# Splits ahead of the gate's chain in head 0, and the norm weight's turn behind x tile 0

## The chip, the cores and the metric

The kernel runs on one core of one Trainium2 chip. The metric is the device time of one execution in microseconds. Before the change the median of three runs is 1736.66 us (1736.09 to 1736.99).

The engines are called TensorE (PE; PEld is its weight load), VectorE (DVE), ScalarE (ACT), GpSimd (POOL) and SyncE (SP). They run side by side, each takes its own instructions in order, and they meet through semaphores.

## The reference, cut to what matters

One layer: RMSNorm, forgetting attention with a residual, RMSNorm, SwiGLU with a residual, and a last RMSNorm. 512 tokens, width 2048, 4 heads of 256, all in float32. This case touches the first norm, the projections of head 0 and the decay of the attention:

```
h    = rmsnorm(x, norm_mix)
proj = h @ w_in                       # q, k, v of 1024 columns each, and 4 gate columns
f    = proj[..., 3*A:] + b_f
cum  = cumsum(log_sigmoid(f), axis=tokens)
logits = (q @ k.T) * HEAD_DIM**-0.5 + cum[t] - cum[s]      # s <= t
o    = softmax(logits) @ v ; x = x + merge(o) @ w_out
```

## The kernel before, in words

**Two parts of each number.** A float32 product is made of three passes over a high and a low part of each operand (fp32r). ScalarE writes the high part as a copy (`split_hi`, L915, instruction at L919), VectorE the low part as raw less high (`split_lo`, L1342, L1344). A **slab** is 128 columns of a weight, 2048 rows deep; `raw` has three places and `split` two. Slab n goes to place n mod 2 of `split`, so its split waits until slab n - 2 is used (`slab_used`), and SP's queue loads slab n + 3 when slab n is split (`lo_ready`).

**Head 0's slabs** are 0 and 1 (q), 2 and 3 (k), 4 and 5 (v). TensorE projects each in 48 matmuls (`project`, L1942; all matmuls of a product have the line L1907) into one of two banks in turn. `take_qk` empties the bank of a q or k slab: VectorE multiplies it in place by the row of roots (L1410; for v the product goes to `vT`), ScalarE copies the high part (L961), VectorE makes the low part (L1419). TensorE's projection j waits for the slab's low part and for take_qk j - 2.

**The opening** (TensorE from L2030, ScalarE from L1007, VectorE from L1458). POOL sets constants. TensorE keeps itself busy with four matmuls (L2017), turns the norm weight's rows (L2034) into a bank, and ScalarE copies that to `gain_col` (L1010, `gain_taken`); this bank is also that of the last two of the 16 chunks of the turned x, so TensorE waits for `gain_taken` ahead of these. `turn_x` (L1924, L1934) turns a tile of 128 tokens of x in 16 transposes; two tiles make a half (EARLY, LATE) of 256 tokens, which ScalarE and VectorE take chunk by chunk, scaled by `gain_col`, into high (`take_x`, L931) and low part (L1358). ScalarE squares each x tile for the root mean square (`square_x`, L1002). The gate's columns `wf` are spread over `pad` in high (L1017) and low part (L1454), and `gate` (L2025) makes the gate's columns out of 16 matmuls for each half. Slab 0 is split in four pieces (L1021, L1459; `first_lo` counts the low ones) and projected for the early half, then the late one; then come slab 1's tiles, with the turn of the row of roots in between (L2058), whose result VectorE copies to `root_row` (L1527).

**The gate's chain** in head 0: `gate_sums` on VectorE, a DMA that moves rows down 16 partitions (`gate_moved`, issued by ScalarE at L1030), then in `gate_decay` (L1489) on VectorE sums, root and bias (L1493 to L1498, `gate_v` 3 to 5), on ScalarE `gate_softplus` (L988: Abs, Exp, Ln with a load of a table), on VectorE minimum, cumulative sum and the two parts of the decay (L1500 to L1517), and `decay_h` (L1431). The scores (`scores`, L1951) need `decay_ready` and four take_qk.

**Who sets the order.** Every engine's order is written out by hand. For head 0 the functions `head` are called with `before=None` (`fresh`); the other heads run in a loop of three, with the work of the head before them between the steps. Behind the heads come w_out, the second norm, and the feed-forward part by Strassen-like products, which takes most of the time.

Of the kernel before, what the change touches and what calls it, by code (L numbers as in the profile page):

```python
# [23 lines left out]
ALU = mybir.AluOpType  # L24
# [148 lines left out]
def fox_layer(nc, x, norm_mix, w_in, b_f, w_out, norm_ffn, w_gu, w_down, norm_out, out):  # L173
# [38 lines left out]
    with ExitStack() as ctx:  # L212
# [6 lines left out]
        def f32(ap):  # L219
            return ap.bitcast(F32)  # L220
# [693 lines left out]
        def _(act):  # L914
# [19 lines left out]
            def softmax(h):  # L934
                for tb in range(NT):
                    act.wait_ge(max_ready, NT * h + (tb + 1))
                    nc.scalar.activation(tmp_row(tb), ps[:, SC[tb], 0:(tb + 1) * P], ACT.Exp,
                                         bias=negmax[:, tb:tb + 1],
                                         accum_out=rowsum[:, tb:tb + 1]).then_inc(exp_done, 1)
# [19 lines left out]
            def take_qk(h, at, j):  # L959
                act.wait_ge(rescaled, QK * h + (j + 1))  # L960
                nc.scalar.activation(qk[j // NH][0][:, j % NH, :], ps[:, PROJ[j % 2], :], ACT.Copy,  # L961
                                     scale=SCALE if j < NH else 1.0).then_inc(qk_hi, 1)

            def head(at, h, before=None):

                fresh = before is None
                if not fresh:
                    split_hi(at.plus(1))
                    softmax(before)
                take_qk(h, at, 0)  # L970
                split_hi(at.plus(2))
                if fresh:
                    gate_softplus()
                if not fresh:
                    take_v(before)
                take_qk(h, at, 1)
                split_hi(at.plus(3))
                if not fresh:
                    take_pT(before)
                take_qk(h, at, 2)  # L980
                split_hi(at.plus(4))
                if not fresh:
                    take_o(before)
                take_qk(h, at, 3)
                split_hi(at.plus(5))
                split_hi(at.plus(6))
# [21 lines left out]
            act.dma_start(gain_rows[0:ND, :], norm_mix.rearrange("a (c p) -> (a c) p", p=P)).then_inc(gain_in, 16)  # L1008
            act.wait_ge(gain_turned, 1)
            nc.scalar.activation(gain_col[:], ps[:, SC[3], 0:ND], ACT.Copy).then_inc(gain_taken, 1)  # L1010
            square_x(0)
            act.wait_ge(gain_taken, 1)
            take_x(0, range(0, 4))
# [4 lines left out]
            take_x(0, range(4, ND))  # L1018
# [322 lines left out]
        def _(dve):  # L1341
# [79 lines left out]

            def head(at, h, head_col, before=None):
                fresh = before is None
                if not fresh:
                    split_lo(at.plus(1))
                    softmax(before)
                take_qk(h, at, 0)
                split_lo(at.plus(2))
                if fresh:
                    gate_decay()  # L1430
                nc.vector.tensor_scalar(decay_h[:], f32(decay_s[:]), head_col, None,  # L1431
                                        ALU.mult).then_inc(decay_ready, 1)
                if not fresh:
                    take_v(before)
                take_qk(h, at, 1)
                split_lo(at.plus(3))
                if not fresh:
                    take_pT(before)
                take_qk(h, at, 2)
                split_lo(at.plus(4))  # L1440
                if not fresh:
                    take_o(before)
                take_qk(h, at, 3)
                split_lo(at.plus(5))
                take_v_rows(h, at, 0)
                split_lo(at.plus(6))
                take_v_rows(h, at, 1)
# [3 lines left out]
            take_x(0, range(0, 4))  # L1451
# [4 lines left out]
            take_x(0, range(4, ND))  # L1456
# [32 lines left out]
            def gate_decay():  # L1489
# [8 lines left out]
                nc.vector.tensor_scalar(z, z, bf[:, 0:1], None, ALU.add).then_inc(gate_v, 1)  # L1498
                dve.wait_ge(gate_s, 3)
# [22 lines left out]
            for tb in range(NT):  # L1522
                dve.wait_ge(rstd_ready, tb + 1)
                nc.vector.tensor_scalar(vT[:, 0, tb * P:(tb + 1) * P], warm[:, 0:P], rstd[:, tb:tb + 1], None,
                                        ALU.add).then_inc(root_spread, 1)
            dve.wait_ge(root_turned, 1)
# [375 lines left out]
        def _(pe):  # L1902
# [129 lines left out]
            pe.wait_ge(const_set, IDENT)  # L2032
            pe.wait_ge(gain_in, 16)
            nc.tensor.transpose(ps[:, SC[3], 0:P], gain_rows, ident[:]).then_inc(gain_turned, 1)  # L2034
            turn_x(0, range(0, ND - 2))
# [6 lines left out]
            turn_x(2, range(0, 2 * FIVE))  # L2042
            for j in range(2):
                pe.wait_ge(first_lo, j + 1)
                project(first, PROJ[0], EARLY, range(4 * j, 4 * j + 4), wait=False)
            turn_x(3, range(0, 2 * FIVE))
            pe.wait_ge(first_lo, 3)
            project(first, PROJ[0], EARLY, range(8, 12), wait=False)
            project(first, PROJ[0], EARLY, range(12, ND))
# [5 lines left out]
            project(first.plus(1), PROJ[1], tiles=range(0, ND // 2))  # L2055
# [4 lines left out]
            project(first.plus(1), PROJ[1], tiles=range(ND // 2, ND)).then_inc(slab_used, 1)  # L2060
# [225 lines left out]
```

## Time and profile before

| | us |
|---|---|
| median of three runs | 1736.66 |
| the profiled run | 1736.89 |
| its span | 1735.1 |
| TensorE busy | 1713.1 (99%) |
| VectorE busy | 1214.6 (70%) |
| ScalarE busy | 780.3 (45%) |
| GpSimd busy | 174.7 (10%) |

Times in the views are microseconds from the start of the span. A busy TensorE isn't TensorE at its peak: matmuls are pipelined, the next starts before the last has ended, so the distance of two starts counts, not the duration of one. The granted clock is given as a share of 2.4 GHz; 0.50 is 1.2 GHz, and a value between says that the clock changed in that stretch. A line of the order of time merges like instructions: start, time from the first start to the last end, engine, line, operation, count, and in brackets how long the engine sat idle ahead of it and who ended that.

### The profile page before, as it was taken

How to read it: one execution, taken by the hardware profiler on the slowest of the kernel's cores; microseconds unless marked ns; L12 is line 12 of the kernel's file. 1: busy time of each engine (PE TensorE's matmuls, PEld its weight loads, DVE VectorE, ACT ScalarE, POOL GpSimd, SP SyncE). 2: the span in 40 equal slices, each digit the busy share in tenths (PEclk: the TensorE clock that was granted, in tenths of full speed). 3: DMA queues.
4: the chain of work that ended last, by engine and by line, in shares of the span. 5: the costliest groups of instructions: out<-in, count | busy, mean ns of one | idle time of the engine just before them, and what ended most of it. 6: DMA issues, size and time to landing. Idle time of an engine off the chain costs nothing.

```text
span 1735.1 us, 24508 instructions
## 1 busy us (share of the span) xinstructions
PE 1713.1 (99%) x8861; PEld 1465.5 (84%) x8861; DVE 1214.6 (70%) x1323; ACT 780.3 (45%) x956; POOL 174.7 (10%) x276
## 2 busy tenths in 40 slices
PE   9899999999999999999999999999999999999997
PEld 7688888888988888888888888888887888888886
DVE  4533434335877777777777777777779978888886
ACT  5222222233344544455454545445455544445454
POOL 1000000000001111111111111111100100000043
PEclk9999999999999999999999999999999999999999
DMA  7233332252347777776777777777778886876854
GB/s 225 73 97 79 91 79 91 73 206 61 92 126 199 180 181 187 205 195 176 186 187 193 181 180 181 208 195 178 184 231 237 255 244 197 249 188 190 254 156 143
DMA packets 306437, 296.44 MB, mean 171 GB/s; under 512 B 9425, under 2 KB 258529, under 8 KB 300753
## 3 DMA queue, kind: packets, MB, share of 16 engines
q1 hardware_dynamic: 288704, 223.67, 42.0%
q0 software_dynamic: 15120, 65.54, 19.6%
q10 hardware_dynamic: 2560, 6.53, 1.1%
q8 instruction: 34, 0.56, 0.1%
q14 instruction: 19, 0.15, 0.0%
HBM read 202.68 MB, written 27.26 MB: 133 GB/s over the span
## 4 chain that ended last, share of the span: by engine, by line
PE 95%; DVE 2%; ACT 1%; issue 1%; POOL 0%; DVEq 0%; POOLq 0%; ACTq 0%
PE ps L2159 30%; PE ps L2210 24%; PE ps L1907 20%; PE ps L2165 16%; PE ps L2143 2%; PE ps L2148 1%; DVE tmp L1369 1%; PE ps L2125 1%; PE ps L2025 1%; PE ps L2017 0%; PE ps L2129 0%; PE ps L1934 0%; DVE split L1344 0%; PE ps L1979 0%; DVE hT L1350 0%
## 5 line engine op out<-in xcount | busy, mean ns | idle before, releaser
L1096 ACT ACTIVATE split<-raw 128x1024 fp32r<-128x1024 f32 x295 | 312.1, 1058 | 342.5 <-DVE raw L1602 112.9
L1591 DVE TENSOR_TENSOR split<-raw,split 128x1024 fp32r<-128x1024 f32 x295 | 360.5, 1223 | 139.0 <-ACT split L1096 134.9
L2210 PE MATMUL ps<-split,operand_hi 128*128 128x512 f32 x1232 | 380.7, 389 | 1.0 <-DVE operand_lo L1746 0.8
L1907 PE MATMUL ps<-hT,split 128*128 128x512 f32 (+1 forms) x1200 | 268.3, 384 | 6.9 <-DVE split L1344 6.9
L2210 PEld LDWEIGHTS ps<-split,operand_hi 128*128 128x128 f32 x1232 | 231.3, 188 | 50.9 <-DVE operand_lo L1746 1.2
L1907 PEld LDWEIGHTS ps<-hT,split 128*128 128x128 f32 x1200 | 219.6, 189 | 50.8 <-issue 7.7
L2159 PE MATMUL ps<-hT,split 128*128 128x512 f32 x984 | 246.4, 392 | 0.0
L2210 PE MATMUL ps<-split,operand_lo 128*128 128x512 f32 x616 | 239.7, 389 | 0.0
L1196 ACT ACTIVATE split<-down_slot 128x2048 fp32r<-128x2048 f32 (+1 forms) x84 | 148.6, 1774 | 179.9 <-PE ps L2210 86.8
L2159 PEld LDWEIGHTS ps<-hT,split 128*128 128x128 f32 x984 | 177.0, 189 | 31.7
L1732 DVE TENSOR_TENSOR split<-down_slot,split 128x2048 fp32r<-128x2048 f32 (+1 forms) x84 | 177.2, 2109 | 20.9 <-ACT split L1196 17.4
L2159 PE MATMUL ps<-oT,split 128*128 128x512 f32 x656 | 164.3, 392 | 0.0
L2165 PEld LDWEIGHTS ps<-hT,split 128*128 128x128 f32 x984 | 134.2, 190 | 9.6
L2165 PE MATMUL ps<-hT,split 128*128 128x256 f32 x984 | 137.2, 282 | 0.0
L2159 PEld LDWEIGHTS ps<-oT,split 128*128 128x128 f32 x656 | 118.0, 189 | 21.1
L2210 PEld LDWEIGHTS ps<-split,operand_lo 128*128 128x128 f32 x616 | 115.7, 188 | 23.8
L1757 DVE TENSOR_TENSOR xres<-xres,ps 128x1024 f32<-128x1024 f32 (+1 forms) x74 | 88.0, 1189 | 42.8 <-PE ps L2210 42.4
L1344 DVE TENSOR_TENSOR split<-raw,split 128x2048 fp32r<-128x2048 f32 x33 | 75.6, 2292 | 53.9 <-ACT split L919 53.9
L1602 DVE TENSOR_TENSOR raw<-raw 128x1024 f32<-128x1024 f32 x83 | 101.7, 1226 | 7.8
L814 POOL TENSOR_TENSOR turn_of<-half 128x1 f32<-128x1 f32 x81 | 31.4, 388 | 740.4 <-DVE raw L1602 316.4
L919 ACT ACTIVATE split<-raw 128x2048 fp32r<-128x2048 f32 x33 | 63.0, 1914 | 84.5 <-PE ps L1907 80.9
L2165 PEld LDWEIGHTS ps<-oT,split 128*128 128x128 f32 x656 | 89.5, 190 | 6.4
(184 smaller groups left out, 1927.7 us busy)
## 6 DMA issues: line engine op xcount, KB each, us to landing
raw<-in_ffn_w_gate_up_dram SPq DMA_DIRECT2D x172, 512.0 KB, 4.8
raw<-raw POOLq DMA_DIRECT2D x81, 512.0 KB, 4.5
down_slot<-in_ffn_w_down_dram SPq DMA_DIRECT2D x32, 1024.0 KB, 7.0
raw<-in_fox_w_in_dram SPq DMA_DIRECT2D x24, 1024.0 KB, 5.7
a_sums<-pack SPq DMA_DIRECT2D x22, 1024.0 KB, 6.3
down_slot<-down_slot POOLq DMA_DIRECT2D x16, 1024.0 KB, 7.6
operand_raw<-a_sums SPq DMA_DIRECT2D x28, 512.0 KB, 6.4
down_slot<-in_ffn_w_down_dram SPq DMA_DIRECT2D x16, 768.0 KB, 5.4
```

Of the source, the lines that this page charges most:

```text
L919: nc.scalar.activation(split[0][:, at.ring, :], raw[:, at.raw, :], ACT.Copy).then_inc(hi_ready, 1)
L1096: nc.scalar.activation(ring(r, 0, n), source, ACT.Copy).then_inc(t_hi, 1)
L1196: nc.scalar.activation(down_ring(dn, 0, e), down_part(dn, DOWN_OF[e]), ACT.Copy).then_inc(d_hi, 1)
L1344: nc.vector.tensor_tensor(split[1][:, at.ring, :], raw[:, at.raw, :], f32(split[0][:, at.ring, :]), ALU.subtract).then_inc(lo_ready, 1)
L1591: nc.vector.tensor_tensor(ring(r, 1, n), source, f32(ring(r, 0, n)), ALU.subtract).then_inc(t_lo, 1)
L1602: nc.vector.tensor_tensor(x1, x1, x2, ALU.add).then_inc(t_sum, 1)
L1732: nc.vector.tensor_tensor(down_ring(dn, 1, e), down_part(dn, DOWN_OF[e]), f32(down_ring(dn, 0, e)), ALU.subtract).then_inc(d_lo, 1)
L1757: nc.vector.tensor_tensor(part, part, down_banks(dn, which)[:, tiles, :], ALU.add if sign > 0 else ALU.subtract).then_inc(y_added, 1)
L1907: ins = nc.tensor.matmul(bank, stationary(sp, t), moving(mp, t), start=first and t == tiles[0] and (sp, mp) == PASSES[0], stop=last and t ...
L2159: ins = nc.tensor.matmul(both, ring(at.r, 0, n)[:, k * P:(k + 1) * P], tokens[2][:, :, k * HALF:(k + 1) * HALF], start=e < 2 and k == 0, s ...
L2165: ins = nc.tensor.matmul(both[:, 0, :], ring(at.r, 1, n)[:, k * P:(k + 1) * P], tokens[0][:, k * HALF:(k + 1) * HALF], start=False, stop=k ...
L2210: ins = nc.tensor.matmul(banks[:, tile, :], operand[e][part][:, i, tile * P:(tile + 1) * P], down_ring(dn, part_of_t, e)[:, i * BANK:(i + ...
```

## The change

Six moves, no work added or taken away:

1. TensorE turns chunks 0 to 13 of x tile 0 ahead of the norm weight, not behind it.
2. ScalarE squares x tile 0 ahead of its copy to `gain_col`; ScalarE and VectorE take two chunks ahead of the pads, not four.
3. TensorE projects pieces j = 0 and 1 of slab 0 ahead of ten transposes of x tile 2 and 3 each, not behind tile 2's.
4. The row of roots is turned behind ten tiles of slab 1, not eight.
5. In head 0 slab 2 is split ahead of take_qk 0, on VectorE ahead of the copy to `root_row` too.
6. The gate's chain goes in two parts: `gate_logits` and ScalarE's `gate_softplus` behind the split of slab 3, the rest (`gate_decay`, and `decay_h`) behind the split of slab 4. Both stood behind slab 2's split, ahead of take_qk 1.

```diff
 # ScalarE, head
+                if fresh:
+                    split_hi(at.plus(2))
                 take_qk(h, at, 0)
-                split_hi(at.plus(2))
-                if fresh:
-                    gate_softplus()
                 if not fresh:
+                    split_hi(at.plus(2))
                     take_v(before)
                 take_qk(h, at, 1)
                 split_hi(at.plus(3))
+                if fresh:
+                    gate_softplus()
 # ScalarE, opening
+            square_x(0)
             act.wait_ge(gain_turned, 1)
             nc.scalar.activation(gain_col[:], ps[:, SC[3], 0:ND], ACT.Copy).then_inc(gain_taken, 1)
-            square_x(0)
             act.wait_ge(gain_taken, 1)
-            take_x(0, range(0, 4))
+            take_x(0, range(0, 2))
...
-            take_x(0, range(4, ND))
+            take_x(0, range(2, ND))
 # VectorE, head
                 take_qk(h, at, 0)
-                split_lo(at.plus(2))
-                if fresh:
-                    gate_decay()
-                nc.vector.tensor_scalar(decay_h[:], f32(decay_s[:]), head_col, None,
-                                        ALU.mult).then_inc(decay_ready, 1)
                 if not fresh:
+                    split_lo(at.plus(2))
+                    decay_of(head_col)
                     take_v(before)
                 take_qk(h, at, 1)
                 split_lo(at.plus(3))
+                if fresh:
+                    gate_logits()
...
                 split_lo(at.plus(4))
+                if fresh:
+                    gate_decay()
+                    decay_of(head_col)
 # VectorE, opening (its two take_x as ScalarE's), and the gate
-            def gate_decay():
+            def gate_logits():
...
                 nc.vector.tensor_scalar(z, z, bf[:, 0:1], None, ALU.add).then_inc(gate_v, 1)
+            def gate_decay():
+
+                dve.wait_ge(gate_v, 5)
                 dve.wait_ge(gate_s, 3)
...
+            split_lo(At(2))
             dve.wait_ge(root_turned, 1)
 # TensorE, opening
+            turn_x(0, range(0, ND - 2))
             pe.wait_ge(gain_in, 16)
             nc.tensor.transpose(ps[:, SC[3], 0:P], gain_rows, ident[:]).then_inc(gain_turned, 1)
-            turn_x(0, range(0, ND - 2))
...
-            turn_x(2, range(0, 2 * FIVE))
-            for j in range(2):
-                pe.wait_ge(first_lo, j + 1)
+            for j in range(4):
+                pe.wait_ge(first_lo if j < 3 else lo_ready, j + 1 if j < 3 else 1)
                 project(first, PROJ[0], EARLY, range(4 * j, 4 * j + 4), wait=False)
-            turn_x(3, range(0, 2 * FIVE))
-            pe.wait_ge(first_lo, 3)
-            project(first, PROJ[0], EARLY, range(8, 12), wait=False)
-            project(first, PROJ[0], EARLY, range(12, ND))
+                if j < 2:
+                    turn_x(2 + j, range(0, 2 * FIVE))
...
-            project(first.plus(1), PROJ[1], tiles=range(0, ND // 2))
+            project(first.plus(1), PROJ[1], tiles=range(0, 10))
...
-            project(first.plus(1), PROJ[1], tiles=range(ND // 2, ND)).then_inc(slab_used, 1)
+            project(first.plus(1), PROJ[1], tiles=range(10, ND)).then_inc(slab_used, 1)
```

## Rows read from the trace of the kernel before

**Rows 1.** The page: the chain that ended last, and the group of projection matmuls.
```profile
PE 95%; DVE 2%; ACT 1%; issue 1%; POOL 0%; DVEq 0%; POOLq 0%; ACTq 0%
...
L1907 PE MATMUL ps<-hT,split 128*128 128x512 f32 (+1 forms) x1200 | 268.3, 384 | 6.9 <-DVE split L1344 6.9
```

**Rows 2.** TensorE's waits: total us, times, longest us.
```profile
PE ps L1907 <- DVE split L1344: 6.9, 2, 6.0
...
PE ps L2210 <- DVE operand_lo L1746: 0.8, 1, 0.8
```

**Rows 3.** TensorE in order of time, 30 to 110 us.
```profile
43.08 5.73 PE L1907 MATMUL ps<-hT,split 128*128 128x512 f32 x24
49.70 11.16 PE L1907 MATMUL ps<-hT,split 128*128 128x512 f32 x48 [0.89 <-DVE split L1344]
...
66.89 35.09 PE L1907 MATMUL ps<-hT,split 128*128 128x512 f32 x144 [6.04 <-DVE split L1344]
101.82 0.22 PE L1907 MATMUL ps<-kT_hi,qT_hi 128*128 128x128 f32 x1
```

**Rows 4.** TensorE by stretches: busy (count), granted clock, DMA share, GB/s.
```profile
13.00:14.00 1.00, 0.72 (x2) 0.76 0.96 388
...
16.52:48.60 32.08, 32.08 (x205) 0.99 0.60 157
...
64.00:65.00 1.00, 0.00 (x0) 0.86 0.00 0
...
71.00:72.00 1.00, 1.00 (x5) 0.72 1.03 251
```

**Rows 5.** VectorE and ScalarE in order of time, 43 to 67 us.
```profile
51.43 0.63 ACT L991 ACTIVATE tmp<-tmp 128x512 f32<-128x512 f32 x1 [4.21 <-DVE tmp L1498]
...
62.52 1.90 ACT L919 ACTIVATE split<-raw 128x2048 fp32r<-128x2048 f32 x1
...
43.37 0.69 DVE L1527 COPY root_row<-ps 128x512 f32<-128x512 f32 x1 [5.19 <-PE ps L2058]
...
47.26 2.29 DVE L1344 TENSOR_TENSOR split<-raw,split 128x2048 fp32r<-128x2048 f32 x1 [1.11 <-ACT split L919]
49.47 0.68 DVE L1493 TENSOR_TENSOR tmp<-tmp 112x512 f32<-112x512 f32 x1
...
54.70 0.69 DVE L1500 SCALAR_TENSOR_TENSOR tmp<-tmp 128x512 f32<-128x512 f32 x1 [3.31 <-ACT tmp L995]
...
61.30 0.69 DVE L1410 TENSOR_TENSOR ps<-ps,root_row 128x512 f32<-128x512 f32 x1
...
64.45 2.29 DVE L1344 TENSOR_TENSOR split<-raw,split 128x2048 fp32r<-128x2048 f32 x1 [1.11 <-ACT split L919]
```

**Rows 6.** TensorE in order of time, 0 to 20 us.
```profile
7.62 3.66 PE L1934 MATMUL ps<-ident,xres 128*128 128x128 f32 x32
13.28 5.50 PE L2025 MATMUL ps<-hT,oT 128*128 128x512 f32 x16 [2.00 <-DVE oT L1454]
18.61 1.25 PE L1934 MATMUL ps<-ident,xres 128*128 128x128 f32 x10
```

**Rows 7.** ScalarE and VectorE in order of time, 0 to 20 us.
```profile
7.82 0.18 ACT L1010 ACTIVATE gain_col<-ps 128x16 f32<-128x16 f32 x1 [4.67 <-PE ps L2034]
...
9.85 1.57 ACT L931 ACTIVATE hT<-ps,gain_col 128x256 fp32r<-128x256 f32 x4
...
10.80 1.66 DVE L1358 SCALAR_TENSOR_TENSOR hT<-ps,gain_col,hT 128x256 fp32r<-128x256 f32 x4 [10.80 <-ACT hT L931]
...
17.79 2.49 DVE L1459 TENSOR_TENSOR split<-raw,split 128x512 fp32r<-128x512 f32 x4
```

**Rows 8.** DMAs, us to landing: x's first two loads, all four, the norm weight's.
```profile
xres<-in_x_dram SPq DMA_DIRECT2D x2, 1024.0 KB, 6.1
...
DMA to landing us min/median/max: 5.0/7.6/8.6
...
tmp<-in_norm_mix_dram ACTq DMA_DIRECT2D x1, 8.0 KB, 5.3
```

More of the change, by code:

```diff
@@ L1420, in take_qk, with decay_of @@
                                                ALU.mult, ALU.subtract).then_inc(qk_done, 1)
+            def decay_of(head_col):
+                nc.vector.tensor_scalar(decay_h[:], f32(decay_s[:]), head_col, None,
+                                        ALU.mult).then_inc(decay_ready, 1)
             def head(at, h, head_col, before=None):
@@ L1450, in _ @@
             dve.wait_ge(gain_taken, 1)
-            take_x(0, range(0, 4))
+            take_x(0, range(0, 2))
             for r in range(4):
@@ L1455, in _ @@
                                         ALU.subtract).then_inc(pad_lo, 1)
-            take_x(0, range(4, ND))
+            take_x(0, range(2, ND))
             for j in range(4):
```

## The prediction

> **What bounds the kernel now.** I read the chain of waits first: TensorE carries 95% of it [rows 1], so only time in which TensorE waits or runs slowly can be won. Next, the waits of TensorE: two waits of its projections for VectorE's splits make 6.9 us, the longest 6.0, and the others after the opening are under a microsecond each [rows 2]. TensorE in order of time puts both in head 0: 0.89 us ahead of the projection of slab 2 at 49.70 and 6.04 us ahead of slab 3's at 66.89 [rows 3]. Last, VectorE and ScalarE in that stretch say why. VectorE takes its instructions in order, and there the whole chain of the gate (49.47 to 61.3) stands between the split of slab 2 and the rescaling at 61.30, behind which ScalarE's high part (from 62.52) and VectorE's low part (from 64.45) of slab 3 are queued [rows 5]. Slab 3 was there long before; TensorE waits for an order, not for work or data.
>
> **What a stall costs.** A full projection is 48 matmuls: 11.16 us from the first start to the last end [rows 3], less one matmul's own 0.38 [rows 1], over 47 is 0.229 us each, 11.0 us each projection. Slab 1's last 24 start at 43.08, so slab 2's could start at 43.08 + 24 x 0.229 = 48.6; they start at 49.70: 1.1 lost. Slab 3's could start at 49.70 + 11.0 = 60.7; they start at 66.89: 6.2 lost. The second stall also costs clock. The granted clock is 0.86 in 64 to 65 us, where it falls to 1.2 GHz, and 0.72 in 71 to 72, where it comes back to 2.4 [rows 4]. The 144 matmuls from 66.89 to the scores at 101.82 take 34.9 us [rows 3] where 144 x 0.229 = 33.0 would do: 1.9 lost. Sum to be had: 1.1 + 6.2 + 1.9 = **9.2 us**.
>
> **Part 1, the opening (x tile 0 ahead of the norm weight).** What moves is 14 transposes ahead of the weight's one on TensorE, and ScalarE's square ahead of its copy gain_col. Of x's loads the quickest took 5.0 us, and the first two have a median of 6.1; so the first, issued at 0.74 into an empty queue, is the one of 5.0, the norm weight takes 5.3 from its issue at 1.43: 5.7 and 6.7, both before TensorE begins to turn at all, at 7.62 less one transpose of 0.11, so 7.51 [rows 6, 8]. So nothing starts sooner on TensorE, and ScalarE squares in the time in which it had sat idle (its idle of 4.67 before 7.82 [rows 7]), about 5.8 to 7.9. But gain_col now waits for 14 transposes. 32 of them take 3.66 us [rows 6], less the 0.27 that one lasts, over 31: 0.11 each. The weight's transpose starts at 7.51 + 14 x 0.11 = 9.05 and ends at 9.32; gain_col goes from 9.36 to 9.54 (at 7.82 before); TensorE, which had not waited here, waits for that bank from 9.2 to 9.66. Four more transposes (the last two of tile 0, two of tile 1) give ScalarE its first chunk at 9.66 + 3 x 0.11 + 0.27 + 0.04 = 10.30, where it began at 9.85 [rows 7]: **0.45 later**. The square that was taken out of the path is worth less than the detour through the bank.
>
> Behind that, ScalarE's and VectorE's sixteen chunks and four pads are the same work in another order (two chunks ahead of the pads, not four). VectorE's run has no gap from 10.80 to slab 0's low pieces at 17.79 [rows 7], and I see no new one, so it ends 0.45 later. The pads are done two chunks (0.8 us) sooner in that run: the early gate matmuls can start at about 12.9 instead of 13.28. Its second half then catches up with the chunks, which come 0.39 us apart (four in 1.66 with the last one's own 0.48 [rows 7]); the last one waits for chunk 15 at 18.33 and starts at 18.44 (before, about 18.38): no gain. The next work is now the projection of pieces 0, where formerly ten transposes covered the time (18.61 to 19.6 [rows 6]). Its low piece is ready at 17.79 + 0.45 + 0.65 = 18.9, so TensorE resumes at 19.0 instead of 18.61, and the transposes and projections behind it are as many as before. **Cost 0.4 us.** Bounds: minus 0.1 (were the bank's detour nothing, the first chunk would still need 18 transposes from 7.62: 7.62 + 17 x 0.11 + 0.27 = 9.75 against 9.85) and plus 1.5 (VectorE's waits for a split of ScalarE's in head 0 are 1.11 [rows 5]; one such gap, opened by the pads' new order, on top). I take 0.4, as each link has a row.
>
> The clock in the opening: it is 0.76 in 13 to 14 us and 0.99 over 16.5 to 48.6 [rows 4], so it fell at about 13.5 and was back at 16.5 + 0.01 x 32.1 / 0.5 = 17; about the first half of the early gate runs at 1.2 GHz although TensorE had only been without work since 11.2, with transposes ahead of that [rows 6]; in head 0 it fell only after 4 us of waiting (60.9 to 64.7). The Trainium skill, "TensorE: Matmul & The Clock Gate", Part 4, says that transposes don't count as TensorE activity in the way of matmuls. The trace agrees with that: an idle of 2.1 us behind transposes was enough. By that rule the clock falls again in the changed opening, although TensorE rests less there. With 1.2 GHz from 13.5 to 17 as before, the gate still ends at the chunk's pace, so this alone doesn't move the sum.
>
> **Part 2, slab 2 split ahead.** The high part waits for the first projection's end (43.08 less four transposes, 0.4, and 24 x 0.229 [rows 3], so 37.2; plus 0.4), and behind it on ScalarE only take_qk 0 is queued, wanted at 46.6. It takes 1.9 us, the low part 2.3 [rows 5]: 37.8 to 42.1. Cover: VectorE's wait of 5.19 us ahead of 43.37 [rows 5]. The row of roots is turned two tiles later, after 10 tiles of slab 1 instead of 8: 6 matmuls x 0.229 = 1.4 later, and with the 0.4 the copy root_row starts at 43.37 + 1.8 = 45.2. Rescale 0.7, ScalarE's copy 0.6, low part 0.7 and three hand-overs bring the first q tile to 47.9. TensorE ends slab 1 at 48.6 + 0.4 = 49.0 and doesn't wait: cover 1.0 us, the 1.1 is won. If that cover failed, each microsecond of it costs one.
>
> **Part 3, the gate's chain in two.** take_qk 1 now follows at once: 49.3 to 51.3; slab 3's high part 50.5 to 52.4, its low part to 54.7. TensorE wants it at 49.0 + 11.0 = 60.0: cover 5.3. Then gate_logits, 1.95 us (49.47 to 51.43 [rows 5]), to 56.6, and ScalarE's softplus with its table load, 3.27 us (51.43 to 54.70), to 59.9; behind it on ScalarE take_qk 2 is queued, for which TensorE's bank is full at 60.2: cover 0.3 and more, as its rescale comes first. take_qk 2 and slab 4's split: 60.2 to 65.7, wanted at 71.0. gate_decay and decay_h, 6.6 us (54.70 to 61.30), go from 65.7 to 72.3; its new wait for gate_s 3 was met at 59.9. Behind it take_qk 3 starts at 72.3 instead of 71.2, and slab 5's low part ends at 77.8, wanted at 82.0: cover 4.2. Decay is wanted by the scores at 93.0. So all five projections run without a pause, and no pause means no fall of the clock: all of 9.2 is won. The DMA that moves the gate's rows is issued at its old place, 0.4 later, and read 5.2 later (54.7, was 49.47). SP's queue loads slab n + 3 when slab n is split: slab 5's load leaves 7 us sooner, the later ones too, so no load becomes late.
>
> **Sum.** 9.2 - 0.4 = 8.8 us. The scores start at 101.82 - 8.8 = 93.0. Behind them every wait is of TensorE for partners that TensorE itself had released, so the shift reaches the end. The profiled run took 1736.89 for a span of 1735.1, 0.23 above the median of 1736.66; 1736.89 - 8.8 = 1728.1, and against the median **1727.9 us**.
>
> **Rivals.**
> A, **the clock falls later in the opening**, and its slow stretch lies on projections that nothing else paces. For it: TensorE works from 12.9 and in small groups. Against: the idle and the transposes end within 0.4 us of where they did. Price: a slow stretch like that of 13.5 to 17 costs half its 3.5 us, 1.7: 1729.6. The skill's rule on transposes in the same section speaks rather for the old place.
> B, **the stall moves**: gate_decay stands ahead of slab 5's split. For it: 6.6 us on a queue that TensorE needs. Against: 4.2 us of cover. It decides when the chain in front gets 4.2 us longer; at double its length TensorE waits 6.6 - 4.2 = 2.4, and the clock may cost the 1.9 again: 1730.3 to 1732.2.
> C, **the edit doesn't do what it says**: slab 3 still comes late because something of the order (softplus ahead of take_qk 2, the table load) holds TensorE as long as before: only the 1.1 is won and 0.4 lost, 1736.0.
> D, **slower: the clock stays at 1.2 GHz through the opening.** With matmuls paced by VectorE at 0.39 us and split up by transposes it might not come back at 17. Each microsecond at half clock costs half a microsecond; it decides from 17.6 us on. Up to slab 1's end (49) it is 32 us, cost 16: 1743.9. Against it: TensorE alternated between transposes and projections from 18.61 on at full clock [rows 4, 6], and all that is changed is one group's place.
>
> **How the numbers follow.** Forecast 0.80, A 0.08, B 0.05, C 0.04, D 0.03. The forecast's own range is 1727.9 with the opening's bounds, 0.5 below and 1.1 above the 0.4, and the 0.9 us over which the three runs of before spread: half of it on either side: 1726.9 to 1729.5. With A (1729.6) under the same spread and the near end of B: 1726.9 to 1730.4. About 0.2%, 3.5 us, is what a measurement of this kernel tells from no change: forecast, A and B are faster (0.93), C the same (0.04), D slower (0.03).
>
> **What would show it.** Opening: gain_col at 9.4, first chunk at 10.3, slab 0's low pieces at 18.2, TensorE waiting twice before the gate. Slab 2's low part done by 42; root_row at 45.2. Slab 2's projection at 49.0, slab 3's at 60.0 with no wait ahead of either, scores at 93.0, granted clock 1.00 from 17 us on. The gate's second part starts at 65.7 and TensorE waits for none of it. The forecast is wrong if TensorE waits anywhere between 19 and 93 us, if the first chunk comes over a microsecond late, or if the clock is at half anywhere behind 17.

## The result and the profile after

The changed kernel takes 1726.94 us (median of four runs, 1726.59 to 1726.96) beside 1736.38 for the kernel before in the same session: ratio 0.9945, 95% interval 0.9933 to 0.9957. That is 9.4 us less where 8.8 was forecast, and it lies at the low edge of the range that I gave. Five later runs of the same kernel gave 1726.80 to 1728.09, so the median of all nine is 1726.96; 43 runs of the kernel before, in the later sessions, have the median 1736.24 (1735.17 to 1737.47). By these the gain is 9.3 us. The profiled run took 1726.96 for a span of 1725.2.

The page: the chain that ended last, which answers to [rows 1], and the projection matmuls.

```profile
PE 97%; DVE 2%; ACT 0%; issue 0%; POOL 0%; DVEq 0%; POOLq 0%; ACTq 0%
...
L1919 PE MATMUL ps<-hT,split 128*128 128x512 f32 (+1 forms) x1200 | 265.8, 382 | 0.1
```

TensorE's waits in the changed kernel (total us, times, longest), which answer to [rows 2]:

```profile
PE ps L2037 <- DVE oT L1462: 1.2, 1, 1.2
PE ps L2219 <- DVE operand_lo L1758: 0.8, 1, 0.8
...
PE ps L1946 <- ACT gain_col L1013: 0.3, 1, 0.3
```

The wait of projections for VectorE's split, 6.9 us before, is gone. A new wait of 0.3 us for `gain_col` is there (ScalarE's copy of the norm weight out of the bank), the one that Part 1 of the prediction named. TensorE in order of time, beside [rows 3, 6] (the row that starts at 47.70 is from a window of its own, from 48 us on, and merges slab 1's last matmuls with four whole projections):

```profile
6.74 1.69 PE L1946 MATMUL ps<-ident,xres 128*128 128x128 f32 x14
8.27 0.27 PE L2047 MATMUL ps<-ident,tmp 128*128 128x128 f32 x1
...
12.21 5.94 PE L2037 MATMUL ps<-hT,oT 128*128 128x512 f32 x16 [1.21 <-DVE oT L1462]
18.25 1.69 PE L1919 MATMUL ps<-hT,split 128*128 128x256 f32 x12
...
27.49 3.90 PE L2037 MATMUL ps<-hT,oT 128*128 128x512 f32 x16
...
47.70 44.36 PE L1919 MATMUL ps<-hT,split 128*128 128x512 f32 x195
91.90 0.22 PE L1919 MATMUL ps<-kT_hi,qT_hi 128*128 128x128 f32 x1
```

From there to the scores TensorE doesn't pause once. They start at 91.90, where they started at 101.82: 9.92 us sooner. Behind them nothing moved: 1735.1 - 101.82 = 1633.3 us before and 1725.2 - 91.90 = 1633.3 after.

VectorE in the same stretch, beside [rows 5]. The reader is to see slab 2's split at 39.19 ahead of `root_row`, and the gate's chain in two pieces: 53.96 behind slab 3's split, 64.84 behind slab 4's (62.63).

```profile
39.19 2.29 DVE L1346 TENSOR_TENSOR split<-raw,split 128x2048 fp32r<-128x2048 f32 x1 [1.29 <-ACT split L919]
44.45 0.69 DVE L1539 COPY root_row<-ps 128x512 f32<-128x512 f32 x1 [2.97 <-PE ps L2067]
...
51.75 2.29 DVE L1346 TENSOR_TENSOR split<-raw,split 128x2048 fp32r<-128x2048 f32 x1 [1.11 <-ACT split L919]
53.96 0.68 DVE L1501 TENSOR_TENSOR tmp<-tmp 112x512 f32<-112x512 f32 x1
...
62.63 2.29 DVE L1346 TENSOR_TENSOR split<-raw,split 128x2048 fp32r<-128x2048 f32 x1 [1.11 <-ACT split L919]
64.84 0.68 DVE L1511 SCALAR_TENSOR_TENSOR tmp<-tmp 128x512 f32<-128x512 f32 x1
...
71.43 0.69 DVE L1412 TENSOR_TENSOR ps<-ps,root_row 128x512 f32<-128x512 f32 x1
...
74.59 2.29 DVE L1346 TENSOR_TENSOR split<-raw,split 128x2048 fp32r<-128x2048 f32 x1 [1.11 <-ACT split L919]
```

The granted clock (busy, count, clock, DMA share, GB/s), beside [rows 4]: neither the dip in the early gate nor the one in head 0 is left.

```profile
13.00:14.00 1.00, 1.00 (x4) 1.00 0.98 395
...
49.00:92.00 43.00, 43.00 (x192) 1.00 0.38 98
```

### The profile page after: what moved, and what is told of

Same layout as the page of the kernel before. It is cut to its first block, busy times and chain, and to the rows that moved or that the text cites. A ratio compares the mean times of both kernels' runs of the same rounds, so it can differ in the third digit from the quotient of the medians.

```text
span 1725.2 us, 24509 instructions
## 1 busy us (share of the span) xinstructions
PE 1710.5 (99%) x8861; PEld 1462.4 (85%) x8861; DVE 1214.5 (70%) x1323; ACT 780.4 (45%) x956; POOL 174.4 (10%) x276
## 4 chain that ended last, share of the span: by engine, by line
PE 97%; DVE 2%; ACT 0%; issue 0%; POOL 0%; DVEq 0%; POOLq 0%; ACTq 0%
PE ps L2168 31%; PE ps L2219 24%; PE ps L1919 21%; PE ps L2174 16%; PE ps L2152 2%; PE ps L2157 1%; DVE tmp L1371 1%; PE ps L2134 1%; DVE hT L1360 0%; PE ps L1946 0%; PE ps L2138 0%; PE ps L2029 0%; PE ps L1991 0%; DVE hT L1352 0%; PE ps L2037 0%
```

## The experiments

**How the traces are compared.** The **warm-up** is the four matmuls with which TensorE keeps itself busy at the start; the **late gate** is the gate's product for the second 256 tokens. Three distances on TensorE split each trace: from its first transpose to the late gate (the opening's own work), from the late gate to the scores (head 0), and from the scores to the end, which is 1633.2 to 1633.4 in all but one trace. All numbers below are differences of the starts in the traces, in us.

| kernel | first transpose | late gate | distance | scores | distance from late gate |
|---|---|---|---|---|---|
| before | 7.51 | 27.76 | 20.25 | 101.82 | 74.06 |
| before, again | 7.57 | 27.82 | 20.25 | 101.90 | 74.08 |
| before, filled | 6.84 | 26.76 | 19.92 | 98.66 | 71.90 |
| opening only | 6.29 | 27.05 | 20.76 | 100.31 | 73.26 |
| head only | 7.23 | 27.15 | 19.92 | 91.56 | 64.41 |
| changed | 6.74 | 27.49 | 20.75 | 91.90 | 64.41 |
| changed, again | 7.79 | 28.55 | 20.76 | 92.97 | 64.42 |
| gate in one piece | 6.32 | 27.08 | 20.76 | 92.91 | 65.83 |
| slab 2 behind | 7.35 | 28.12 | 20.77 | 95.03 | 66.91 |
| root at 8 | 7.88 | 28.63 | 20.75 | 93.05 | 64.42 |
| weight first | 6.76 | 27.06 | 20.30 | 91.47 | 64.41 |
| warm-up 3 | 5.78 | 26.89 | 21.11 | 91.30 | 64.41 |
| warm-up 3, turns first | 6.36 | 26.77 | 20.41 | 91.16 | 64.39 |
| warm-up 2, turns first | 5.63 | 26.34 | 20.71 | 90.75 | 64.41 |

**Head only.** The edit to the changed kernel: its opening is taken back to that of before (here without VectorE's two take_x lines and TensorE's order of slab 0's pieces, which are taken back too).

```diff
-            square_x(0)
             act.wait_ge(gain_turned, 1)
             nc.scalar.activation(gain_col[:], ps[:, SC[3], 0:ND], ACT.Copy).then_inc(gain_taken, 1)
+            square_x(0)
...
-            take_x(0, range(0, 2))
+            take_x(0, range(0, 4))
...
-            turn_x(0, range(0, ND - 2))
             pe.wait_ge(gain_in, 16)
             nc.tensor.transpose(ps[:, SC[3], 0:P], gain_rows, ident[:]).then_inc(gain_turned, 1)
+            turn_x(0, range(0, ND - 2))
```

> The changed kernel with the opening of before (norm weight ahead of x tile 0, square behind the copy, four chunks ahead of the pads, slab 0's pieces behind tile 2's transposes); the root's turn behind ten tiles, slab 2's early split and the gate's two parts stay. Theory H (the head's order is all the gain, and the opening's own order is worth nothing or costs): 9.6 us under the kernel before, about 1726.8, first transpose at 7.5 us, early gate partly at 1.2 GHz, scores at 92.1. Rival O (the opening's order brought what stands beyond the forecast, 0.7 us): about 1727.6, scores at 92.9.

Measured: 1727.03 us (1726.12 to 1727.43). TensorE's start and its late gate:

```profile
7.23 0.27 PE L2046 MATMUL ps<-ident,tmp 128*128 128x128 f32 x1
...
27.15 3.90 PE L2037 MATMUL ps<-hT,oT 128*128 128x512 f32 x16
```

Its first transpose is 0.49 later than the changed kernel's and its late gate 0.34 earlier. So the old opening does its work in 0.83 us less, when the clock doesn't dip, and the head's order alone gives 74.06 - 64.41 = 9.65 us. The time equals the changed kernel's within the spread of the runs, and the 1726.8 of theory H is 0.2 away. In three details theory H missed: the first transpose was to come at 7.5, the early gate was to run partly at 1.2 GHz (the granted clock is 1.00 throughout), and the scores were to start at 92.1, where they start at 91.56.

**Opening only.** The reverse: the kernel before with the changed opening (the same lines, in the other direction, and TensorE's order of slab 0's pieces).

> The kernel before with the new opening alone; its head 0 has the old order, root's turn behind eight tiles, the gate's chain whole behind slab 2's split. Theory H: both stalls stand (1.1 and 6.2 us, clock at half after the second). Total within 0.5 us of before: 1736.1 if the clock in TensorE's warm-up rises early again (first transpose at 6.7 us), 1736.8 if it rises as before (first transpose at 7.5, first chunk at 10.3, slab 0's low pieces at 18.2). Rival O: 1735.7 or less and the first transpose at 6.7, since the new order itself brings it forward.

Measured: 1736.88 us (1735.51 to 1737.61, ten runs) beside 1736.1 for before: ratio 1.0002 (0.9992 to 1.0012). Both stalls stand:

```profile
7.82 0.27 PE L2035 MATMUL ps<-ident,tmp 128*128 128x128 f32 x1
8.37 2.19 PE L1934 MATMUL ps<-ident,xres 128*128 128x128 f32 x18 [0.27 <-ACT gain_col L1011]
...
48.99 11.16 PE L1907 MATMUL ps<-hT,split 128*128 128x512 f32 x48 [0.89 <-DVE split L1344]
66.19 34.28 PE L1907 MATMUL ps<-hT,split 128*128 128x512 f32 x144 [6.04 <-DVE split L1344]
```

The profiled run is the fastest of the ten (1735.51) and has its first transpose at 6.29, so that one run alone would have spoken for rival O; the median of ten is on the slower side of the kernel before. The opening's new order brings nothing that the times can show.

**The two again.** To see whether TensorE's early start was the order's doing, both kernels were profiled once more with not a line changed.

> The kernel before, unchanged, profiled once more. In its first trace TensorE's fourth warm-up matmul ran at half clock to the end and the transposes began at 7.5 us. Theory (the moment at which the warm-up speeds up differs from run to run and has nothing to do with the code): it may begin anywhere from 6.3 to 7.9 here, and the late gate follows 20.0 to 20.3 us behind it. Rival (the code's order sets it): 7.5 again, late gate at 27.76.

> The changed kernel, unchanged, profiled once more and timed beside the kernel before. Theory: the first transpose is at another time than 6.74 us and the late gate starts 20.75 us behind it; the time of many runs centres at 0.5 over its first four, 1727.0 to 1727.4, spread over about 2 us. Rival (the order of the opening makes the clock rise early): 6.74 again, all runs within 0.4 of 1726.9.

Measured: before again 1737.02 us, first transpose at 7.57. Changed again 1727.38 us (1726.80 to 1728.09, five runs), and its profiled run:

```profile
7.79 1.69 PE L1946 MATMUL ps<-ident,xres 128*128 128x128 f32 x14
...
28.55 3.90 PE L2037 MATMUL ps<-hT,oT 128*128 128x512 f32 x16
```

The same program starts to turn 1.05 us later than in its first trace, its late gate comes 20.76 behind that, and its scores at 92.97, where the forecast had them (93.0). So the early start of the first trace wasn't the order's doing; what it depends on is in the last section.

**Weight first, and the pieces' order.** Of the three moves in the opening one is undone alone:

```diff
 # the changed kernel, ScalarE and TensorE
-            square_x(0)
             act.wait_ge(gain_turned, 1)
...
+            square_x(0)
...
-            turn_x(0, range(0, ND - 2))
             pe.wait_ge(gain_in, 16)
             nc.tensor.transpose(ps[:, SC[3], 0:P], gain_rows, ident[:]).then_inc(gain_turned, 1)
+            turn_x(0, range(0, ND - 2))
```

> The changed kernel with the norm weight turned ahead of x tile 0 again and ScalarE's copy ahead of its square; two chunks ahead of the pads and the new order of slab 0's pieces stay. Split of the opening by the traces so far: ScalarE's first chunk comes 2.34 us behind TensorE's first transpose in the old order and 2.83 in the new one, the late gate 17.58 behind the first chunk in the old order of pads and pieces and 17.92 in the new. So the late gate 20.26 behind the first transpose here, against 20.76 in the changed kernel and 19.92 in the old opening: 0.5 better than the changed kernel at the same warm-up. Rival (the square behind the copy delays the chunks just as much): 20.7.

Measured: 1727.27 us (1726.60 to 1727.61), not to be told from the changed kernel by time. By the trace the late gate is 20.30 behind the first transpose, not 20.76; ScalarE's first chunk is at 9.12, 2.36 behind a first transpose at 6.76:

```profile
5.75 0.19 PEld L2029 LDWEIGHTS ps<-decay_s 128*128 128x128 f32 x1 [0.24 <-issue]
6.73 0.14 PEld L2046 LDWEIGHTS ps<-ident,tmp 128*128 128x128 f32 x1 [0.79 <-issue]
...
7.09 0.18 ACT L1012 ACTIVATE gain_col<-ps 128x16 f32<-128x16 f32 x1 [3.95 <-PE ps L2046]
7.17 1.90 ACT L1004 ACTIVATE oT<-xres 128x2048 fp32r<-128x2048 f32 x1
...
9.12 0.84 ACT L931 ACTIVATE hT<-ps,gain_col 128x256 fp32r<-128x256 f32 x2
```

Counted from the first transpose, turning x tile 0 ahead of the weight costs 0.46 us, as the prediction's 0.45. But the first transpose isn't quite the same event in both orders. With the weight first, TensorE can't begin before the weight has landed, at about 6.7, and the idle of 0.79 us ahead of 6.73 is in keeping with that; with x first it began at 6.29 in "opening only" and at 6.32 in "gate in one piece". So when the warm-up ends early, most of the 0.46 comes back (an estimate: 6.7 + 20.30 = 27.0 with the weight first, 27.05 in "opening only").

**Three warm-up matmuls.** `stay_warm(4, SC[3])` becomes `stay_warm(3, SC[3])` in the changed kernel.

> The changed kernel with three warm-up matmuls instead of four. If the warm-up's end is what x tile 0 waits for (it landed at 5.7 us, the transposes began at 6.7), TensorE turns from about 5.9 us, but the norm weight lands at 6.7 and ScalarE's square ends at 7.7, so its chunks start at 9.3 instead of 9.57: 0.2 to 0.3 us less, 1726.7. Rival: with less work ahead the clock is at 1.2 GHz in the gate and perhaps the projections behind it: 0.5 to 2 us more, 1727.5 to 1729.

Measured: 1726.32 us (1726.20 to 1726.47), with the closest runs of all. It is 0.6 under the changed kernel, and all four runs lie below the nine of that one, but they are of another session; the ratios to the kernel before, 0.9941 (0.9925 to 0.9958) and 0.9945, don't tell the two apart. In this trace the landing of x sets the start, not the warm-up:

```profile
5.78 1.72 PE L1946 MATMUL ps<-ident,xres 128*128 128x128 f32 x14 [0.20 <-DMA xres<-in_x_dram]
...
26.89 3.90 PE L2037 MATMUL ps<-hT,oT 128*128 128x512 f32 x16
```

**Three, and the turns first.** The old order of slab 0's pieces on top of that:

```diff
-            stay_warm(4, SC[3])
+            stay_warm(3, SC[3])
...
-            for j in range(4):
-                pe.wait_ge(first_lo if j < 3 else lo_ready, j + 1 if j < 3 else 1)
+            turn_x(2, range(0, 2 * FIVE))
+            for j in range(2):
+                pe.wait_ge(first_lo, j + 1)
                 project(first, PROJ[0], EARLY, range(4 * j, 4 * j + 4), wait=False)
-                if j < 2:
-                    turn_x(2 + j, range(0, 2 * FIVE))
+            turn_x(3, range(0, 2 * FIVE))
+            pe.wait_ge(first_lo, 3)
+            project(first, PROJ[0], EARLY, range(8, 12), wait=False)
+            project(first, PROJ[0], EARLY, range(12, ND))
```

> The changed kernel with three warm-up matmuls and with TensorE's old order of slab 0's pieces (ten transposes of tile 2 ahead of pieces 0). In the traces so far the late gate starts 17.58 us behind ScalarE's first chunk with that order and 17.92 with the changed one; the first chunk comes at 8.97 with three warm-up matmuls. So the late gate at 26.55 instead of 26.89, 0.3 under the run with three matmuls alone: 1726.0. Rival (the pieces' order is neutral, the 0.34 is the pads' order): 1726.3.

Measured: 1726.18 us (1725.92 to 1726.64), the lowest median, though not apart from 1726.32. In its trace the warm-up sped up later, and the first chunk is at 9.20; the late gate is 17.57 behind that:

```profile
9.20 0.84 ACT L931 ACTIVATE hT<-ps,gain_col 128x256 fp32r<-128x256 f32 x2 [0.81 <-PE ps L1946]
...
26.77 3.91 PE L2037 MATMUL ps<-hT,oT 128*128 128x512 f32 x16
```

So the pieces' order is the 0.34 us (17.92 in the changed kernel), and the pads behind two chunks instead of four are worth nothing (17.57 with two, 17.58 with four, in "head only"): the rival named for this run, the pads, fell by the trace. By the times it can't be told.

**Two warm-up matmuls, turns first.** As the last, with `stay_warm(2, SC[3])`.

> The changed kernel with two warm-up matmuls and the old order of slab 0's pieces. The warm-up then ends ahead of the landing of x tile 0 at 5.7 us whatever its clock: transposes from 5.8, first chunk at 8.97, late gate at 26.55 in every run, so 1726.0 with a spread of no more than 0.3. Rival (TensorE is too little at work ahead, the clock is at 1.2 GHz for the gate and the projections of slab 0): 1.7 us and more over it, 1727.7.

Measured: 1727.01 us, from 1725.81 to 1727.84. The profiled run is the fastest of all and has its late gate at 26.34, better than the 26.55 expected, with the clock at 1.00 throughout. But two of the four runs took 1.9 and 2.0 us more. That is about what the rival gave for a stretch at half clock in the opening; those runs have no trace, so this is an inference. The expected even spread is refuted: by these four runs three matmuls are the safer choice.

**Slab 2 behind take_qk 0.** In the changed kernel the early split is undone, on both engines:

```diff
-                if fresh:
-                    split_hi(at.plus(2))
                 take_qk(h, at, 0)
+                split_hi(at.plus(2))
                 if not fresh:
-                    split_hi(at.plus(2))
...
-            split_lo(At(2))
```

> The changed kernel with slab 2's split behind take_qk 0 again, on ScalarE and VectorE (the gate's chain stays in two parts behind slabs 3 and 4, the root's turn behind ten tiles). Theory (cover is what counts): root_row at 44.5 us, take_qk 0 to 47.2, slab 2's high part to 48.3, its low part to 50.7, where TensorE wants it at 48.3: a stall of 2.5 us ahead of slab 2 and none later, 2.5 over the changed kernel, 1729.4. Rival (the early split is of no account, the gate's move is all): no stall, 1726.9. Rival (the stall costs clock as the long one did): 1730.5 to 1731.5.

Measured: 1729.69 us (1728.94 to 1730.13).

```profile
51.42 43.77 PE L1916 MATMUL ps<-hT,split 128*128 128x512 f32 x192 [2.24 <-DVE split L1344]
```

The distance from the late gate to the scores is 66.91, 2.50 over 64.41: the stall expected, to the tenth, and the granted clock is 1.00 behind the pause of 2.2 us. The median is 2.75 over the changed kernel's, 0.3 over the 1729.4 expected.

**The gate in one piece behind slab 3.**

```diff
                 if fresh:
                     gate_logits()
+                    gate_decay()
+                    decay_of(head_col)
...
                 split_lo(at.plus(4))
-                if fresh:
-                    gate_decay()
-                    decay_of(head_col)
```

> The changed kernel with the gate's chain whole behind slab 3's split (logits, wait for ScalarE's softplus, decay), ahead of take_qk 2. This doubles the chain ahead of slab 4's split. By the cover worked out in the trace: logits end at 55.9, softplus at 59.2, decay at 65.8, take_qk 2 to 67.9, slab 4's low part at 71.4; TensorE wants it at 70.1: a stall of 1.4 us and no fall of the clock, 1728.3. If the covers are of no account (rival: an order on VectorE costs what it takes), the 6.6 us come back in full with the clock: 1735. If cover is wider than thought: 1726.9 as it is.

Measured: 1728.82 us (1728.02 to 1728.93).

```profile
71.06 22.01 PE L1918 MATMUL ps<-hT,split 128*128 128x512 f32 x96 [1.16 <-DVE split L1346]
```

Late gate to scores 65.83, 1.42 over the changed kernel where 1.4 was worked out; the median is 1.9 over it, 0.5 over the 1728.3 expected. So 6.6 us of VectorE's work cost 1.4 us here and nothing one slab later; rival B's mechanism is real, and its cover is as wide as computed.

**Root at 8.** `range(0, 10)` and `range(10, ND)` of slab 1 become `range(0, ND // 2)` and `range(ND // 2, ND)`.

> The changed kernel with the row of roots turned behind eight tiles of slab 1, as before. Theory: slab 2's split ends at 41.5 us and the roots come at 42.7 then, both off TensorE's path: no change against the changed kernel within the spread of runs, 1726.9, TensorE without a wait. Rival (the copy to root_row and the split collide on VectorE, and TensorE waits ahead of slab 2): 0.5 us or more over it.

Measured: 1727.11 us (1726.50 to 1728.09). TensorE runs from the roots to the scores without a wait (distance 64.42), so this move is free and wasn't needed:

```profile
43.96 49.25 PE L1919 MATMUL ps<-hT,split 128*128 128x512 f32 x216
```

**Before, filled.** To weigh the clock by itself, the kernel before gets idle work in its long stall:

```diff
+                if fresh:
+                    filled = ps[:, SC[1], :].rearrange("p (n t) -> p n t", n=2)
+                    for _ in range(24):
+                        nc.tensor.matmul(filled, h_ffn[0][:, 0, 0, 0:P], h_both[:, :, 0, 0, :], start=True, stop=True)
                 for j in range(3, PER_HEAD):
```

> The kernel before with 24 more matmuls of 512 columns into a bank that nobody reads there, queued on TensorE behind slab 2's projection: they fill 5.5 us of the wait of 6.2 ahead of slab 3 and add nothing to the result. Theory (part of the stall's price is the clock): slab 3 starts when it did, but its matmuls run at 2.4 GHz at once; the 144 matmuls to the scores take 32.7 us instead of 34.9: 2.0 us less than before, 1734.3 beside 1736.3. Rival (the slow first matmuls have another reason, such as the projection's own start): no change, 1736.3.

Measured: 1733.78 us (median of ten, 1733.63 the lowest) beside 1736.28: ratio 0.9988 (0.9978 to 0.9997).

```profile
59.66 5.60 PE L2012 MATMUL ps<-hT 128*128 128x512 f32 x24
65.92 32.90 PE L1907 MATMUL ps<-hT,split 128*128 128x512 f32 x144 [0.65 <-DVE split L1344]
98.66 0.22 PE L1907 MATMUL ps<-kT_hi,qT_hi 128*128 128x128 f32 x1
```

From slab 3's start to the scores it is 32.74 us, where [rows 3] had 101.82 - 66.89 = 34.93. Slab 3 starts 39.16 behind the late gate, where it started 39.13 behind it before: only what follows has changed. Work that no one reads takes 2.2 us off this stretch, and the medians differ by 2.5: the clock's share of the long stall is shown.

This trace is of the slowest of the ten runs, 1737.60, and is the one whose end isn't 1633.3 behind its scores but 1637.1. TensorE waited 1.92 us for a split of w_out at 360 us, and behind that pause the clock fell: it is 0.57 over the next 4 us, which costs 0.43 x 4 = 1.7 us. The two make 3.6 of the 3.8; without the 3.8 this run would be at the median. It doesn't touch the rows above.

```profile
360.02 40.22 PE L1907 MATMUL ps<-split,oT 128*128 128x512 f32 x169 [1.92 <-DVE split L1344]
```

```profile
356.00:358.00 2.00, 2.00 (x10) 1.00 1.05 406
358.00:360.00 2.00, 0.10 (x1) 1.00 1.05 397
360.00:364.00 4.00, 3.98 (x10) 0.57 1.03 406
```

## Why the prediction was right, and where it missed

**In short.** The mechanism of the gain was right: both stalls and the slow stretch in head 0 went, and the opening gave none of it. Two steps of the sum failed. The head's term, 9.2, measured 9.65: a matmul was priced at 0.229 us instead of 0.227, and with it the clock's share of the long stall at 1.9 instead of 2.2. And Part 1 took TensorE's start at 7.51 as a constant, also in its bounds; with four warm-up matmuls this start lay anywhere from 6.29 to 7.88. At an equal start the gain is 9.65 - 0.5 = 9.15 us, beside 9.3 by all the runs; the 9.4 of the first four may have some luck of the start in it.

**The head (Parts 2 and 3): right in each step, 0.45 short in size.** No pause, no fall of the clock. The moments came 0.6 to 0.9 us sooner than forecast, mostly because TensorE's start was 0.77 sooner; the covers are what was foretold. Forecast and traced: slab 2's low part at 42.1 and 41.5; the cover ahead of slab 2's projection 1.0 (its q tile is done at 46.54 + 0.69 = 47.2, TensorE comes at 48.3); slab 3's low part 54.7 and 54.0; the gate's second part from 65.7 and 64.8; slab 5's low part 77.8 and 76.9, with 4.1 us of cover (4.2). The stretch from the late gate to the scores is 9.65 us shorter than in both traces of the kernel before, wherever the head is the changed one and nothing in it is undone; 9.2 was forecast. (Beside "opening only", which has the old head, it is 8.85 shorter: the slow stretch was shorter there.) The term that was mis-sized is the matmul's: I took one projection's first start to last end, less 0.38, over 47: 0.229 us. In "slab 2 behind" the 192 matmuls from 51.42 to the scores at 95.03 take 43.6 us, 0.227 each. That makes the projections 0.1 us shorter each and the clock's share 34.93 - 32.74 = 2.2 us, not 1.9; the stalls are 1.2 and 6.3, together 9.7.

**The opening (Part 1): the mechanism right, the starting point not.** The step that failed is "before TensorE begins to turn at all, at 7.62 less one transpose of 0.11, so 7.51". I took the warm-up's end of one trace as a constant. It was 6.74 in the first trace of the changed kernel and 7.79 in the second, so gain_col (8.58, for 9.36), first chunk (9.57, for 10.30) and late gate (27.49, 0.27 sooner for 0.4 later) came 0.67 to 0.78 sooner than forecast. At the same start the changed opening takes 20.75 from first transpose to late gate, where the one of before took 20.25: a cost of 0.5 for a forecast 0.4. Of this, 0.46 is the weight behind x tile 0 and 0.34 the pieces' order, less 0.33 that the clock's dip had cost before (20.25 in the kernel before, 19.92 with the same opening where the clock didn't dip). The first trace's 9.92 us are 9.65 from the head, 0.77 from an earlier start, less 0.5. So the order of the opening isn't part of the gain, although x tile 0 ahead of the weight reads as one half of the change.

**The clock in the opening: wrong.** I wrote that it would fall in the early gate as before. It fell in none of the ten traces in which TensorE waits 1.2 us ahead of the gate (the changed opening and its variants), and of the four traces with the old one, which wait 2.0, in two (before and before again; not head only nor filled). It changed little, as VectorE's chunks pace the gate's second half either way: the last gate matmul waits for chunk 15, as computed. The Trainium skill, "TensorE: Matmul & The Clock Gate", Part 4, says that transposes don't count as TensorE activity in the way of matmuls. By that rule nothing counted lay between the warm-up and the gate in either opening, and the clock should have fallen in both. The traces don't bear that out as I used it; what the clock counts stays open.

**The rivals.** A: no slow stretch on the projections of the changed kernel in any trace. B: refuted for the change; where the chain in front was made longer ("gate in one piece"), it cost 1.4, without the clock's 1.9. C and D: nothing of either.

## What to carry to other kernels

When an engine with an order of its own holds up the next operand by a long chain that is wanted late, move the operand's step ahead of the chain and cut the chain where it waits for another engine anyway. Add up for each piece when it is wanted: here 6.6 us behind slab 4 cost nothing and the same 6.6 behind slab 3 cost 1.4. And before a change of under a microsecond in the first microseconds is called a gain, profile the same kernel twice: measure from an event such as the first transpose, not from the start of the span, and see whether the edit itself changes what that event waits for, as the weight's landing here.

## What the runs showed of the hardware

**The warm-up speeds up at a moment that differs from run to run.** TensorE's weight loads in the warm-up come 0.85 us apart at first and 0.43 apart later. That is a ratio of two, and I read it as 1.2 and 2.4 GHz; the granted clock is shown as 1.00 all along, so the profile doesn't confirm it. The kernel before, first trace, where it didn't come before the last ones:

```profile
4.89 0.34 PEld L2017 LDWEIGHTS ps<-decay_s 128*128 128x128 f32 x1 [0.52 <-issue]
5.74 0.34 PEld L2017 LDWEIGHTS ps<-decay_s 128*128 128x128 f32 x1 [0.52 <-issue]
6.59 0.25 PEld L2017 LDWEIGHTS ps<-decay_s 128*128 128x128 f32 x1 [0.52 <-issue]
```

The changed kernel, first trace, with the same code on TensorE up to there, where it came at about 5.2:

```profile
4.89 0.32 PEld L2029 LDWEIGHTS ps<-decay_s 128*128 128x128 f32 x1 [0.52 <-issue]
5.45 0.19 PEld L2029 LDWEIGHTS ps<-decay_s 128*128 128x128 f32 x1 [0.24 <-issue]
5.88 0.19 PEld L2029 LDWEIGHTS ps<-decay_s 128*128 128x128 f32 x1 [0.24 <-issue]
```

In eleven traces with four warm-up matmuls the first transpose came at 6.29 to 7.88 us. That is 1.6 us, beside the 1.5 over which the nine runs of the changed kernel spread and the 2.3 of the 43 of the kernel before; between the two traces of the changed kernel the start differs by 1.05 and the time by 1.13. With three matmuls, whose end the landing of x at about 5.7 covers in one trace and not in the other (first transpose at 5.78 and 6.36), four runs lay within 0.3 and four of the other order within 0.7. The Trainium skill, "TensorE: Matmul & The Clock Gate", section "What's actually happening", says of this clock that the chip's own timing doesn't start anew with the kernel; the two traces of the changed kernel, 6.74 and 7.79, are in keeping with that.

**After a pause of about 2 us the clock may or may not be lost.** The granted clock stayed at 1.00 after pauses of 1.2 and 2.2 us in head 0 (gate in one piece, slab 2 behind). It also did after the 2.0 us ahead of the early gate in "head only" and "before, filled". But it fell after the same 2.0 us in both traces of the kernel before, and after 1.92 us ahead of w_out in "before, filled". So a pause of this length can't be priced from one trace. What decides isn't shown.

After the 6.0 us pause the slow stretch cost 2.2 us in the kernel before and 0.8 less in "opening only" (34.12 us for the 144 matmuls, not 34.93). The pause is the same, but in "opening only" the clock fell sooner, at 62.3, 2.2 us behind TensorE's last matmul, and was back sooner, at 69.1, 2.9 us behind slab 3's first matmul; in the kernel before it fell at 64.7, 3.9 us behind the last one, and was back at 71.6, 4.7 behind slab 3's first. These moments are worked out from the granted clock of stretches of 1 to 4 us, such as this one of "opening only":

```profile
60.00:64.00 4.00, 0.15 (x1) 0.79 0.00 0
...
69.00:70.00 1.00, 1.00 (x6) 0.94 1.15 348
```
